# A causal convolution's third running sum: from VectorE multiply-adds to ScalarE products added by accumulating transfers

## The reference, cut to what matters

```
a, b = split(u)                        # 512 positions x 256 channels each
h = a * sigmoid(b)
h = causal depthwise conv(h, 31 taps) + cv_b
h = silu(layernorm over channels(h) * ln_w + ln_b)
```

## Time and profile before

| | |
|---|---|
| median of 3 runs | 1370.57 us (1369.55 to 1372.21) |
| the profiled execution's own time | 1373.39 us |
| its span | 1371.8 us |
| TensorE busy | 1279.7 us (93%) |
| VectorE busy | 861.9 us (63%) |
| ScalarE busy | 572.3 us (42%) |
| GpSimd busy | 103.7 us (8%) |
| software DMA queue | 11.69 MB, 4.9% of 16 engines' span |
| hardware DMA queue q1 | 134.40 MB, 32.8% |

### The profile page before, as it was taken

The page is one execution under the profiler, slowest core; times in us unless marked ns, Lnnn a source line. Parts: engine busy times, 40 slices in busy tenths (PEclk is TensorE's granted clock), DMA queues, the critical chain, the costliest instruction groups (busy, mean ns, idle before and its releaser), DMA issues.

```text
span 1371.8 us, 18899 instructions
## 1 busy us (share of the span) xinstructions
PE 1279.7 (93%) x6581; PEld 1024.9 (75%) x6581; DVE 861.9 (63%) x1297; ACT 572.3 (42%) x802; POOL 103.7 (8%) x154
## 2 busy tenths in 40 slices
PE   6799688999899999999999999999999989999797
PEld 2677566788688788788888887887788867777576
DVE  4679798757765322444444887764466567888753
ACT  3365443552444211333333655542233335467532
POOL 6014330000000000000000000010011000100000
PEclk9899899999899999999999999999999989999899
DMA  8577982324545333333322232333232312322131
GB/s 297 142 208 150 183 167 64 122 64 138 169 123 166 94 92 93 91 94 105 92 92 77 77 112 70 87 90 101 77 89 82 105 54 85 103 73 84 34 104 61
DMA packets 209910, 147.85 MB, mean 108 GB/s; under 512 B 7683, under 2 KB 192178, under 8 KB 209857
## 3 DMA queue, kind: packets, MB, share of 16 engines
q1 hardware_dynamic: 200784, 134.40, 32.8%
q0 software_dynamic: 6848, 11.69, 4.9%
q10 hardware_dynamic: 2224, 1.05, 0.3%
HBM read 135.06 MB, written 2.10 MB: 100 GB/s over the span
## 4 chain that ended last, share of the span: by engine, by line
PE 63%; DVE 17%; issue 7%; ACT 6%; DMA 5%; POOL 1%; DVEq 0%; ACTq 0%; SPq 0%; POOLq 0%
PE banks L392 19%; PE banks L394 19%; PE banks L393 19%; ACT w_hi L364 2%; DVE w_lo L376 2%; DMA raw<-in_ada_w 1%; DMA cacc<-rstd 1%; DMA cacc<-sqb 1%; DVE t_s L2278 1%; DVE xc L2258 1%; DMA omix<-rstd 1%; DVE score L1776 1%; DVE m L1773 1%; DVE score L1759 1%; POOL e L2438 1%
## 5 line engine op out<-in xcount | busy, mean ns | idle before, releaser
L392 PE MATMUL banks<-h_hi,w_hi 128*128 128x512 f32 x824 | 334.1, 405 | 19.7 <-issue 4.7
L376 DVE TENSOR_TENSOR w_lo<-raw,w_hi 128x1024 fp32r<-128x1024 f32 x204 | 249.8, 1231 | 149.4 <-ACT w_hi L364 145.5
L393 PE MATMUL banks<-h_lo,w_hi 128*128 128x512 f32 x824 | 326.0, 396 | 0.0
L394 PE MATMUL banks<-h_hi,w_lo 128*128 128x512 f32 x824 | 325.5, 395 | 0.0
L364 ACT ACTIVATE w_hi<-raw 128x1024 fp32r<-128x1024 f32 x204 | 213.4, 1053 | 156.7 <-PE banks L394 137.5
L392 PEld LDWEIGHTS banks<-h_hi,w_hi 128*128 128x128 f32 x824 | 158.0, 192 | 62.2 <-issue 13.4
L393 PEld LDWEIGHTS banks<-h_lo,w_hi 128*128 128x128 f32 x824 | 158.1, 192 | 34.3 <-issue 2.4
L394 PEld LDWEIGHTS banks<-h_hi,w_lo 128*128 128x128 f32 x824 | 157.8, 191 | 34.1
L392 PE MATMUL banks<-n_hi,w_hi 128*128 128x512 f32 x256 | 102.5, 400 | 3.6 <-DVE h_lo L2207 2.4
L392 PE MATMUL banks<-hid_hi,w_hi 128*128 128x512 f32 x256 | 102.2, 399 | 0.0
L393 PE MATMUL banks<-hid_lo,w_hi 128*128 128x512 f32 x256 | 101.7, 397 | 0.0
(11 more groups left out here) (381 smaller groups left out, 1846.2 us busy)
## 6 DMA issues: line engine op xcount, KB each, us to landing
raw<-in_mlp_w SPq DMA_DIRECT2D x64, 512.0 KB, 3.9
raw<-in_a_w_in SPq DMA_DIRECT2D x48, 512.0 KB, 3.9
raw<-in_ada_w SPq DMA_DIRECT2D x40, 512.0 KB, 4.6
raw<-in_w_in SPq DMA_DIRECT2D x28, 512.0 KB, 4.5
raw<-in_b_w_in SPq DMA_DIRECT2D x24, 512.0 KB, 3.8
raw<-in_a_w_out SPq DMA_DIRECT2D x16, 512.0 KB, 3.6
raw<-in_b_w_out SPq DMA_DIRECT2D x16, 384.0 KB, 3.2
raw<-in_w_out SPq DMA_DIRECT2D x8, 512.0 KB, 4.3
```

The source lines that it names most:

```text
L376: dve.tensor_tensor(dst, src, hi, ALU.subtract).then_inc(split_lo, 1)
L392: pe.matmul(dst, l_hi, r_hi, start=first, stop=False)
L393: pe.matmul(dst, l_hi, r_lo, start=False, stop=False)
L394: return pe.matmul(dst, l_lo, r_hi, start=False, stop=last)
```

## The change

THIRD_TAPS, THIRDS_AT and `third_tap` are gone. All 30 taps 1 to 30 are products of ScalarE. Of each tile, tap 0 is written into "even", tap 1 into "odd", tap 2 into "third", and the other 28 come by accumulating transfers, into the three sums by turns. PRODUCTS_AT now has four products in each of the slots 6 to 19, two in 5 and two in 20; before it had two or three in each of 5 to 19. The ring of four buffers is the same. The transfers and `join` wait for the semaphores' new counts.

```diff
--- before.py
+++ after.py
@@ -119,12 +119,9 @@
              13: [(1, 2)], 14: [(1, 2)], 15: [(1, 2)], 16: [(1, 2)], 17: [(1, 2)], 18: [(2, 3)], 19: [(2, 3)], 20: [(2, 3)],
              21: [(2, 3), (3,)], 22: [(2, 3), (3,)], 23: [(2, 3), (3,)], 24: [(3,)], 25: [(3,)], 26: [(3,)], 27: [(3,)]}
 assert all(sum(b in r for rs in ROUNDS_AT.values() for r in rs) == TOPK // 8 for b in (1, 2, 3))
-THIRD_TAPS = [k for k in range(1, TAPS) if k % 3 == 0]
-SENT_TAPS = [k for k in range(1, TAPS) if k % 3]
-PRODUCTS_AT = {5: 2, 6: 3, 7: 3, 8: 2, 9: 2, 10: 2, 11: 2, 12: 3, 13: 3, 14: 3, 15: 3, 16: 3, 17: 3, 18: 3, 19: 3}
-THIRDS_AT = {6: 3, 7: 3, 8: 2, 9: 2, 16: 2, 17: 2, 18: 2, 19: 2, 20: 2}
+SENT_TAPS = list(range(1, TAPS))
+PRODUCTS_AT = {5: 2, 6: 4, 7: 4, 8: 4, 9: 4, 10: 4, 11: 4, 12: 4, 13: 4, 14: 4, 15: 4, 16: 4, 17: 4, 18: 4, 19: 4, 20: 2}
 N_PRODUCTS = CVT * len(SENT_TAPS)
-assert sum(THIRDS_AT.values()) == CVT * len(THIRD_TAPS)
 assert sum(PRODUCTS_AT.values()) == N_PRODUCTS
 N_LEVELS, N_NEAR, BLOCK = 8, 6, 32
 U_LEVEL, U_MEAN, U_ATT = 15, 22, 23
@@ -434,15 +431,14 @@
             return (sqb[:, 0, :], sqb[:, 1, :], ssq[:, :], rstd[:, :])[n % 4]
 
         third, odd = omix[:, 4:6, :], omix[:, 6:8, :]
-        PER_M = len(SENT_TAPS) - 1
-        EVEN_PER_M, ODD_PER_M = (PER_M + 1) // 2, PER_M // 2
+        PER_M = len(SENT_TAPS) - 2
+        SUM_PER_M = [len(range(s, PER_M, 3)) for s in range(3)]
 
         def sum_of(n):
 
             m, j = divmod(n, PER_M)
-            if j % 2:
-                return odd_summed, odd, m * ODD_PER_M + j // 2
-            return even_summed, cacc, m * EVEN_PER_M + j // 2
+            summed, into = ((even_summed, cacc), (odd_summed, odd), (third_summed, third))[j % 3]
+            return summed, into, m * SUM_PER_M[j % 3] + j // 3
 
         block = ctx.enter_context(nc.Block())
 
@@ -1275,10 +1271,11 @@
                     act.wait_ge(conv_gated, m + 1)
                     act.activation(cacc[:, m, :], hpad[:, m, 0:TOK], ACT.Identity, bias=pcol("cv_b", m), scale=pcol("cv_w", m))\
                        .then_inc(first_tap, 1)
-                    act.activation(odd[:, m, :], hpad[:, m, k:k + TOK], ACT.Copy, scale=pcol("cv_w", CVT * k + m))\
+                if j < 2:
+                    act.activation((odd, third)[j][:, m, :], hpad[:, m, k:k + TOK], ACT.Copy, scale=pcol("cv_w", CVT * k + m))\
                        .then_inc(first_tap, 1)
                     return
-                n = m * PER_M + j - 1
+                n = m * PER_M + j - 2
                 if n >= 4:
                     summed, _, o = sum_of(n - 4)
                     act.wait_ge(summed, 16 * (o + 1))
@@ -1895,25 +1892,13 @@
                 dve.scalar_tensor_tensor(omix[:, h, :], hk[:, h, :], hon[:, h:h + 1], banks[:, SPREAD_BANKS[h], :],
                                          ALU.mult, ALU.mult).then_inc(oa_made, 1)
 
-            def third_tap(n):
-
-                m, j = divmod(n, len(THIRD_TAPS))
-                k = THIRD_TAPS[j]
-                src, w = hpad[:, m, k:k + TOK], pcol("cv_w", CVT * k + m)
-                if j == 0:
-                    dve.wait_ge(conv_gated, m + 1)
-                    dve.tensor_scalar(third[:, m, :], src, w, None, ALU.mult).then_inc(third_summed, 1)
-                else:
-                    dve.wait_ge(third_summed, n)
-                    dve.scalar_tensor_tensor(third[:, m, :], src, w, third[:, m, :], ALU.mult, ALU.add).then_inc(third_summed, 1)
-
             def join(m):
 
-                dve.wait_ge(odd_summed, 16 * ODD_PER_M * (m + 1))
-                dve.wait_ge(third_summed, len(THIRD_TAPS) * (m + 1))
+                dve.wait_ge(odd_summed, 16 * SUM_PER_M[1] * (m + 1))
+                dve.wait_ge(third_summed, 16 * SUM_PER_M[2] * (m + 1))
                 dve.tensor_tensor(third[:, m, :], third[:, m, :], odd[:, m, :], ALU.add).then_inc(joined, 1)
                 dve.wait_ge(joined, m + 1)
-                dve.wait_ge(even_summed, 16 * EVEN_PER_M * (m + 1))
+                dve.wait_ge(even_summed, 16 * SUM_PER_M[0] * (m + 1))
                 dve.tensor_tensor(cacc[:, m, :], cacc[:, m, :], third[:, m, :], ALU.add).then_inc(tapped, 1)
 
             def slot(u):
@@ -1932,9 +1917,6 @@
                     level(u - U_LEVEL - 1)
                 for r in ROUNDS_AT.get(u, ()):
                     top_round(r)
-                done = sum(c for v, c in THIRDS_AT.items() if v < u)
-                for n in range(done, done + THIRDS_AT.get(u, 0)):
-                    third_tap(n)
                 if u in (U_ATT - 5, U_ATT - 1):
                     join((u - U_ATT + 5) // 4)
                 if u == U_ATT:
@@ -2390,11 +2372,11 @@
             def add_product(n):
 
                 m, j = divmod(n, len(SENT_TAPS))
-                if j == 0:
+                if j < 2:
                     return
-                n = m * PER_M + j - 1
+                n = m * PER_M + j - 2
                 summed, into, o = sum_of(n)
-                pool.wait_ge(first_tap, 2 * m + 2)
+                pool.wait_ge(first_tap, 3 * m + 3)
                 pool.wait_ge(weighted, n + 1)
                 if o:
                     pool.wait_ge(summed, 16 * o)
```

## The result

The changed kernel takes 1383.05 us (median of 4 runs, 1382.32 to 1385.42), the kernel before beside it 1370.06 (1367.32 to 1372.21): 13.0 us more. The ratio of the two, as it is computed over the runs, is 1.0100, with a 95% interval of 1.0083 to 1.0117. The forecast was 1379.1, between 1372 and 1390, and slower.

What follows compares the result with a forecast made beforehand. The prediction took nearly full DMA engines, with accumulations beside weight loads, to bound the middle of the convolution's stretch. Slots 11 to 16 (+9.4) and 17 to 20 (-0.9) gave +8.5 us on the 1370.6 median: 1379.1, range 1372 to 1390.

Steps and rivals of the forecast that it cites:

- What an accumulation costs: One 256 KB accumulating transfer takes 1.57 us of full DMA engines, beside 1.9 us for a weight load.
- A third sum fills the gaps: Three transfers in flight keep the DMA engines 97% full in slots 11 to 16, but make no transfer shorter.
- Slots 6 to 10: VectorE's slots with ten removed taps: slot 11 starts at 135.5 us against 135.60 before, so nothing is gained.
- relief and delay even: The 5.7 us VectorE gains from removed early taps are eaten by its waits before slots 9 to 11.
- the sum: The forecast's addition of accumulations, weight loads and waits by groups of slots: +9.4 - 0.9 = +8.5 us.
- drained queue: 1.5 us added before slot 11 because GpSimd is held twice by masks until VectorE's scores are there.
- Slots 11 to 16: 22 accumulations and 6 weight loads, 45.9 us, at 97% full 47.3; slot 17 starts 9.4 us later, at 182.8.
- Slots 17 to 20: Slot 19 starts 19.0 us after slot 17, slot 21 starts 34.2 after it against 35.1 before: -0.9 us.
- From the profiled execution to the median: The profiled execution (1373.4 us) was 2.8 over the median (1370.6), so the forecast became 1379.1 instead of 1381.9.
- The point of no change: A rival: an accumulation takes 1.35 us, packed, and slot 11 comes two us earlier, giving 1370.3 us; chance 0.14.
- Rival one: Transfers of three sums overlap and four products hide in a slot: -20 us, 1350.6 us; chance 0.10.
- the loop behind slot 17: VectorE's update, ScalarE's read-out, products and high half: 15.3 us for two slots, 31 for four against 35.

Runs made afterwards that it cites:

- e1: Changed kernel with each accumulating transfer cut to half its columns (128 KB), same number and order of transfers: 1365.44 us, ratio 0.9965 to the kernel before.
- e4: Changed kernel with each accumulating transfer cut to 512 bytes on one partition, same issues and waits: 1358.70 us, ratio 0.9919 to the kernel before.
- e9: Changed kernel with each transfer a plain copy into its sum instead of an addition: 1367.60 us, ratio 0.9961 to the kernel before.
- e2: Changed kernel with the same 56 transfers going by turns into two sums instead of three: 1396.31 us, ratio 1.018 to the kernel before.
- e7: Kernel before with VectorE's third taps moved into slots 10 to 16 and ScalarE's products placed otherwise: 1364.35 us, ratio 0.9947.

## Why the prediction was right

The sign and the cause hold; the size was forecast too small, 8.5 us for 13.0. By its steps:

- *What an accumulation costs* (1.57 us of full engines): right, 1.57 and 1.59. e1, e4 and e9 show that it is this time that makes the kernel slower: with 0.90, about none and 0.69 us for one, all else equal, it is faster than the kernel before.
- *A third sum fills the gaps* (97% full, not 79%): right, 98.6% and 99.9%, and e2 shows the alternative, 85% and 13 us more.
- *Slots 6 to 10* (slot 11 at 135.5, relief and delay even): **mis-sized**. Slots 6 to 10 took 43.8 us in the sum (135.5 less 91.67) and 46.0 and 47.2 in fact. The sum had 16 accumulations and one weight load a slot, 25.1 + 9.5 us, and 1.5 us of drained queue. The first accumulation went out 4.8 us after slot 6's start, as the sum has it. From 99.7 us, its issue, to the landing at 139.2 us for which slot 10's last product and slot 11's high half wait, the two queues had 71.4% and 28.6% of the engines: no drained queue, but 4.64 MB or 17.7 accumulations (28.2 us) and 3.06 MB or 5.8 loads (11.3 us). More loads than one a slot and part of the accumulations behind the sixteenth were served in it. From 95 to 110 us alone the hardware queue had 50.5% of the engines and the software queue 34.4%, 0.84 MB or some three accumulations in 15 us (rows below); in slot 7 ScalarE's last product stood 4.58 us for the transfer that was issued at 105.47 and took 7.35 us (chain, above).

```profile
q1 hardware_dynamic: 3864, 1.95, 50.5%
q0 software_dynamic: 460, 0.84, 34.4%
```

- *Slots 11 to 16* (47.3 us, +9.4): 45.5 and 45.0, and +8.3 against the mean of two profiles of before. Slot 17 came 91.1 us after slot 6 in the sum, 91.5 and 92.2 in the traces: the two errors cancel, and that is luck. The queues were fuller here than the 97% of the sum (98.6% and 99.9%).
- *Slots 17 to 20* (-0.9): -0.8. Slot 19 starts 17.2 us after slot 17 here, not 19.0, and slot 21 16.2 after that, not 15.2; again the sum held and not its parts, by luck. The forecast's own terms, besides, give 18.8 for its 19.0, and 27.3 + 8.1 - 1.5 = 33.9 for its 34.2. The joins began at 200.4 and 236.6 us (197.8 and 236.7 in the second profile), where the forecast had near 198 and 233.
- *From the profiled execution to the median*: **a doubtful step, and its size is open**. By the profiled execution the forecast was 1381.9, by the median, 2.8 lower, 1379.1; measured was 1383.05. I took the whole 2.8 us off the time after. Where the engines' work sets the time anew, a longer stretch in the profile of before must not be taken off once more. The two profiles of before are 6.0 us apart (1373.39 and 1367.39), of which 2.6 lie ahead of slot 6, 2.2 in slots 6 to 16 (81.7 against 79.5) and 1.2 behind. So some 1 to 2 of the 2.8 us may lie in the stretch that the change rules; two profiles don't show it. What can be said by stretches: slots 6 to 20 gave +10.4 us by the table's means, where the sum had +8.5, mostly because the one profile of before that the sum started from was longer there (116.8 us against 114.0 in the second). The other 2.6 of the 13.0 us lie outside these slots, and their cause stays open.
- *The point of no change*, an accumulation of 1.35 us: the runs at 0.90 and 1.57 us lie on either side of it, none nearer. A straight line between these two would put it at 1.1 us, an estimate from their -5.4 and +13.0 us. Below 0.90 us other things set the pace in part: from there to none only 7 us are left (e4), and e9, at 0.69 us, is no faster than e1.
- *Rival one's price* (-20): e4 gives -12. Against the first profile of before it has -6.2 us in slots 6 to 10, -5.4 in 11 to 16 and -1.8 in 17 to 20, where the rival had -5.7, -10.4 and -4. So the loop behind slot 17 holds 2 us more than I let it, and the larger part, 5 us, is in slots 11 to 16: VectorE still stands 3.3 us for high halves there, and its low half of slot 11 took 2.97 us in place of 1.22.

## What to carry to other kernels

Before work is moved from an engine to transfers, add up what the transfers take of the DMA engines, per slot and beside the weights, from the shares of a full stretch; more of them in flight fills gaps only up to 100%. In an in-order list put first what others wait for and last what may wait for a ring: that alone gave 8 us in the kernel before and 11 in the changed one. And look whether the work can go to where its own engine waits; in e7 that lengthened those slots by 5 us and shortened the others by 15.

## What the runs showed that I had not expected

- An accumulating transfer of 256 KB within SBUF takes 1.57 us of full DMA engines, a plain copy of the same bytes 0.69 us; half the bytes, accumulated, 0.90 us. The Trainium skill ("DMA: Bandwidth & Descriptors", Bandwidth) has 435 GB/s for such transfers. By the measurements here the copy, at 380 GB/s, comes near; the accumulation, at 167, does not.
- VectorE's waits for high halves rose from 17.7 to 39.1 us while the kernel lost 13: an engine with less to do waits longer for the same things, so the sum of its waits is no measure of the loss.
- The granted clock went down as well: over 140 to 190 us the mean was 0.80 after and 0.90 before, with TensorE busy for 31.8 and 36.0 of the 50 us (in the second profiles 0.78 and 0.90, busy 32.4 and 38.5). No run here takes it apart from the rest; since ScalarE's read-out of unit 18 came 11.7 us after slot 17's start (186.34 to 198.03), earlier than the 13.3 of before, it shows no cost at that place.

```profile
140.00:190.00 50.00, 31.84 (x365) 24.43 (x363) 31.33 (x66) 29.50 (x43) 23.27 (x27) 0.80 1.00 190
```

(The changed kernel, busy time by engine in the stretch: TensorE, its weight loads, VectorE, ScalarE, GpSimd; then the granted clock, the DMA share and GB/s.)
